# Two fp32 transformer blocks on one core: half of the weight remainders of 16 units made by an adding DMA from GpSimd's queue

## The chip, the cores and the metric

The kernel runs on 1 core of a Trainium2 chip. The metric is device time in microseconds (us), lower is better; the time of a kernel is the median of its runs.

## What is computed

Two blocks follow each other on one sequence of 256 tokens, model width 1024, all in fp32. The stretch that matters here is mixer 1, between the first and the second SwiGLU feed-forward of block one:

```python
proj = h @ w_in                       # c_q 256, c_kv 128, k_rope 32, conv_in 3*512, gates 2*1024
q  = rms_norm(c_q) @ w_uq;  kv = rms_norm(c_kv) @ w_ukv
q, k = per-head rms_norm, rope        # 8 heads, 64 + 32 wide
o_attn = causal softmax attention(q, k, v)
o_conv = gate_b * causal_conv3(gate_c * xv)
merged = sum(sigmoid(gate_logits) * (branches @ w_branch));  y = merged @ w_out
```

After it come the second feed-forward, then block two (attention of two kinds, an MLP, a gated embedding, a final norm).

## The kernel before, in words

**Weights.** The weights come from HBM in *units* of at most 128 x 2048 fp32 (1 MB). `Sync.load` puts unit i into one of four raw buffers (`raw`, slot i % 4, NR = 4). TensorE multiplies in fp32r, so each weight is split into a rounded part ("hi") and a remainder ("lo"). `Scalar.hi` copies both halves of a unit from `raw` into `ring[.., 0, ..]` as fp32r (two activations). `Vector.lo` makes `ring[.., 1, ..] = raw - hi`, one instruction for each half, p = 0 and p = 1. The ring has four slots too (NS = 4): `hi` of weight unit w waits until TensorE has used unit w - 4. Each 128x128 tile then takes three matmuls (`product`), and a tile of the second half waits for `("lo", w, 1)`. A raw buffer is loaded again when both remainders of its unit are made.

Units of a second kind ("ada") hold rows of the modulation matrix. They share the raw buffers; VectorE alone reads them (`Vector.ada`, line L205, tile `sb_junk`, two instructions for each).

**Order.** `Plan` writes one list of steps, and every engine runs its own steps of that list in order. `take_unit` issues `hi` and puts the unit's remainder pieces at the end of a list `pend`; `piece` takes the first piece of it out and puts it into the plan (the load that reuses the raw buffer is planned when the last piece of a unit is out). Pieces go out in four ways: `need` takes units up to three ahead of the one that TensorE begins, and before each of them empties `pend` down to AHEAD = 3 entries; `went` lets one piece go at each fourth tile (PACE = 4), if more than KEEP = 2 are waiting; `fill` lets one go at chosen places between other VectorE work; and `need` forces the pieces of the unit that TensorE is about to use.

```python
        if self.lead and self.tiles // PACE > before // PACE and len(self.pend) > KEEP and not self.hold:
            self.piece()
```

**Mixer 1.** Weight units 33 and 34 are c_q, c_kv and k_rope; 35 and 36 conv_in 1 and 0; three ada units; 37 queries (1536 wide), 38 keys and values (1024 wide); 39 conv_out 0; 40 and 41 conv_in 2 and 3; 42 conv_out 2; 43 to 50 the gates, with ada units ahead of 46, 47 and 48; then the branch and output matrices. GpSimd makes the normalising factors of c_q, c_kv and k_rope in small steps (`Gpsimd.c_factors`). VectorE's statistics of the heads (`head_sums`, `head_factors`) need those factors. They stand in the plan between the keys of unit 38 and the first tile of unit 39. In the plan before, the piece (unit 40, p = 0) stands ahead of these statistics (it goes out at the PACE place of the keys, where four pieces wait), and (unit 40, p = 1) directly behind them. From `conv_out 2` on, the heads' transposes (`turn_heads`, `turned_heads`) and then the attention (`scores_1`, `masked_1`, `exp_1`, `normal_1`, `turn_1`, `turned_1`) run tile by tile beside the projections.

A line number in the rows is mostly that of a helper: L193 ACT activation, L196 tensor_tensor, L217 matmul, L220 transpose.

Of the kernel before, what the change touches and what calls it, by code (L numbers as in the profile page):

```python
# [8 lines left out]
F32, F32R, I32, BF16 = mybir.dt.float32, mybir.dt.float32r, mybir.dt.int32, mybir.dt.bfloat16  # L9
# [4 lines left out]
NR, NS = 4, 4  # L14
# [100 lines left out]
ADA_3 = [5, 6, 9, 17]  # L115

PACE, AHEAD, KEEP = 4, 3, 2
TAKE_AFTER = (1, 2, 3)
SUMS_AT = (1, 3)

# [57 lines left out]
class Engine:  # L178
# [40 lines left out]
    def transpose(self, o, i, ident):  # L219
        return Issued(self.e and self.e.transpose(o, i, ident))  # L220

    def dma_start(self, o, i):
        return Issued(self.e and self.e.dma_start(o, i))


class Turn:
# [238 lines left out]
class Plan:  # L465
# [20 lines left out]
    def load(self):  # L486
        if self.loads < len(self.m.units):
            self.add("load", self.loads)
            self.loads += 1

    def take_unit(self):
        i = self.taken
        self.taken += 1
        kind, blocks = self.m.units[i]
        if kind == "ada":
            self.pend += [("ada", i, b, n) for b, (_, n, _, _) in enumerate(blocks)]
        else:
            w = self.m.windex[i]
            self.add("hi", i, w)
            self.pend += [("lo", i, w, p) for p in range(2)]  # L500

    def fill(self, n=1):
        for _ in range(0 if self.hold else n):
# [167 lines left out]
    def first_ffn(self):  # L671
# [28 lines left out]
        for k in range(8):  # L700
# [13 lines left out]
            for j in range(8):  # L714
                for i in range(2):
                    self.mm(128, "up", "f1", j, k, i, bk[j])
                if k == 7:
                    if j in TAKE_AFTER:
                        self.take_unit()
# [20 lines left out]
    def mixer_1(self):  # L740
# [113 lines left out]

        cut = M1_ORDER.index(("qkv", 0))
        run(M1_ORDER[:cut], SUMS_AT)
        ko = ko[0]

# [86 lines left out]
        self.in_tiles(KEYS_AT, head_keys)  # L945
        self.in_tiles(ATTENTION_AT, start)
        run(M1_ORDER[cut + 1:])
        self.finish_side()
        self.add("gcol", 1, 0.5)
# [363 lines left out]
class Sync(Program):  # L1313


    def run(self):
        steps = {"load_c": self.load_c, "load_con": self.load_con, "load_x": self.load_x, "load": self.load,
                 "load_rows": self.load_rows, "load_mask": self.load_mask, "load_tables": self.load_tables,
                 "bias_store": self.bias_store, "load_bias": self.load_bias, "load_p": self.load_p,
                 "store": self.store, "end": self.end}  # L1320
        for name, args in self.plan.steps:
            if name in steps:
                steps[name](*args)
# [15 lines left out]
    def load(self, i):  # L1339
        m, e = self.m, self.e  # L1340
        if i >= NR:
            kind, blocks = m.units[i - NR]
            if kind == "ada":
                e.wait_ge(*self.at("ada", blocks[-1][1]))
            else:
                e.wait_ge(*self.at("lo", m.windex[i - NR], 1))
        w = m.widths[i]
        src = m.wts[m.offs[i]:m.offs[i] + 128 * w].rearrange("(p w) -> p w", p=128)
        e.dma_start(m.raw[:, i % NR, 0:w], src).then_inc(*self.up(f"unit{i % NR}_in", ("unit", i), by=16))
# [521 lines left out]
class Scalar(Program):  # L1871


    def run(self):
        steps = {"hi": self.hi, "silu_c": self.silu_c, "square_0": self.square_0, "rbc": self.rbc, "h_hi": self.h_hi,
                 "silu": self.silu, "hid_hi": self.hid_hi, "rope_sin": self.rope_sin, "hx_hi": self.hx_hi,
                 "square": self.square, "shift_hi": self.shift_hi, "c_shift": self.c_shift,
                 "c_square": self.c_square, "c_hi": self.c_hi, "c_sums_out": self.c_sums_out,
                 "conv_shift": self.conv_shift, "conv_xs": self.conv_xs, "conv_gate_shift": self.conv_gate_shift,
                 "conv_hi": self.conv_hi, "gate_shift": self.gate_shift, "gate_tanh": self.gate_tanh,  # L1880
                 "q_out": self.q_out, "qr_out": self.qr_out, "v_out": self.v_out, "k_out": self.k_out,
                 "head_squares": self.head_squares, "heads_kr": self.heads_kr, "turned_heads": self.turned_heads,
                 "exp_1": self.exp_1, "turned_1": self.turned_1, "o_hi_1": self.o_hi_1, "merged_hi": self.merged_hi,
                 "shifts": self.shifts, "gate_silu": self.gate_silu, "kA_square": self.ka_square,
                 "vA_out": self.va_out, "qA_square": self.qa_square, "turned_2": self.turned_2, "exp_A": self.exp_a,
                 "turned_pA": self.turned_pa, "o_hi_A": self.o_hi_a, "B_out": self.b_out, "vB_out": self.vb_out,
                 "exp_B": self.exp_b, "turned_pB": self.turned_pb, "o_hi_B": self.o_hi_b,
                 "gate2_tanh": self.gate2_tanh, "sum_hi_2": self.sum_hi_2, "up_out": self.up_out, "down_out": self.down_out, "hid2_hi": self.hid2_hi,
                 "p_hi": self.p_hi, "ple_tanh": self.ple_tanh, "x_square": self.x_square, "x_out": self.x_out,
                 "final_square": self.final_square,  # L1890
                 "final": self.final}
        for name, args in self.plan.steps:
            if name in steps:
                steps[name](*args)

    def hi(self, i, w):
        m, e = self.m, self.e
        e.wait_ge(*self.at("unit", i))
        if w >= NS:
            e.wait_ge(*self.at("used", w - NS))  # L1900
        for p in range(2):
            a, b = m.half(w, p)
            e.activation(m.ring[:, w % NS, 0, a:b], m.raw[:, i % NR, a:b]).then_inc(
                *self.up("weights_hi", ("hi", w, p)))
# [442 lines left out]
class Vector(Elementwise):  # L2347
# [76 lines left out]
    def rsqrt(self, v, z, a, event):  # L2424

        e = self.e
        self.ts(z.bitcast(I32), v.bitcast(I32), -0.5, ALU.mult, 1597463007.0, ALU.add)
        s = 1.0
        for n in range(3):
            e.wait_ge(*self.last())  # L2430
            self.tt(a, z, z, ALU.mult)
            e.wait_ge(*self.last())
            self.tt(a, a, v, ALU.mult)
            e.wait_ge(*self.last())
            e.scalar_tensor_tensor(z, a, 3.0 * s * s, z, ALU.subtract, ALU.mult).then_inc(
                *self.up("vector_own", *([event] if n == 2 else [])))
            s = -2.0 * s ** 3
        assert s == Z_SCALE
# [654 lines left out]
class Gpsimd(Elementwise):  # L3093
# [1 line left out]
    steps_done = "pool_own"  # L3095

    def run(self):
        steps = {"token_factor": self.token_factor, "diagonal": self.diagonal, "c_factors": self.c_factors}
        for name, args in self.plan.steps:
            if name in steps:  # L3100
                steps[name](*args)

    def rsqrt(self, v, z, a, event):

# [182 lines left out]
```

## Time and profile before

| | |
|---|---|
| median of 3 runs | 1026.38 us (1023.08 to 1027.05) |
| the profiled execution | 1024.29 us |
| its span in the profile | 1022.5 us |
| TensorE (matmul) busy | 983.3 us, 96% |
| VectorE busy | 780.2 us, 76% |
| ScalarE busy | 534.1 us, 52% |
| GpSimd busy | 10.5 us, 1% |

The span is the stretch that the profiler's rows cover; the run's own time is 1.8 us more. A busy TensorE is one with a matmul in flight. Units 35 to 50 are used between about 225 us and 345 us of the span.

### The profile page before, as it was taken

How to read it: one execution, taken by the hardware profiler on the slowest of the kernel's cores; microseconds unless marked ns; L12 is line 12 of the kernel's file. 1: busy time of each engine (PE TensorE's matmuls, PEld its weight loads, DVE VectorE, ACT ScalarE, POOL GpSimd, SP SyncE). 2: the span in 40 equal slices, each digit the busy share in tenths (PEclk: the TensorE clock that was granted, in tenths of full speed). 3: DMA queues.
4: the chain of work that ended last, by engine and by line, in shares of the span. 5: the costliest groups of instructions: out<-in, count | busy, mean ns of one | idle time of the engine just before them, and what ended most of it. 6: DMA issues, size and time to landing. Idle time of an engine off the chain costs nothing.

```text
span 1022.5 us, 17350 instructions
## 1 busy us (share of the span) xinstructions
PE 983.3 (96%) x7020; PEld 917.1 (90%) x7020; DVE 780.2 (76%) x1446; ACT 534.1 (52%) x936; POOL 10.5 (1%) x32
## 2 busy tenths in 40 slices
PE   4999999998888999999999999999999999999996
PEld 3999998997887999999998988789999988988895
DVE  5999998978986787685877588556768877677665
ACT  4444654436376555353565445664555654455453
POOL 0000000004000000000000000000000000000000
PEclk9999999999999999999999999999999999999998
DMA  8997999854473555768664445354355555545421
GB/s 305 358 343 281 336 345 342 304 196 167 173 280 124 199 195 182 246 220 206 254 247 165 170 160 203 127 170 143 136 192 169 191 181 192 206 165 194 156 104 41
DMA packets 33277, 213.92 MB, mean 209 GB/s; under 512 B 3757, under 2 KB 6189, under 8 KB 8494
## 3 DMA queue, kind: packets, MB, share of 16 engines
q1 hardware_dynamic: 33198, 212.83, 58.8%
q8 instruction: 55, 0.90, 0.3%
q14 instruction: 24, 0.20, 0.0%
HBM read 210.19 MB, written 2.62 MB: 208 GB/s over the span
## 4 chain that ended last, share of the span: by engine, by line
PE 85%; DVE 7%; ACT 3%; issue 2%; DMA 1%; POOL 1%; SPq 0%; DVEq 0%; ACTq 0%; POOLq 0%
PE bank L217 84%; DVE sb_ring L196 2%; PE bank L220 2%; DMA sb_raw<-wts 1%; ACT sb_ring L193 1%; ACT sb_tmp L193 1%; DVE sb_tq L196 1%; DVE sb_tmp L202 1%; DVE sb_tmp L196 1%; DVE sb_junk L205 1%; ACT R L193 0%; DVE sb_nst L196 0%; DVE sb_tmp L199 0%; POOL sb_st_a L196 0%; DVE R L196 0%
## 5 line engine op out<-in xcount | busy, mean ns | idle before, releaser
L217 PE MATMUL bank<-sb_h,sb_ring 128*128 128x258 f32 (+2 forms) x3776 | 495.0, 291 | 8.7 <-DVE sb_ring L196 4.0
L217 PEld LDWEIGHTS bank<-sb_h,sb_ring 128*128 128x128 f32 x3776 | 474.1, 189 | 23.0 <-issue 4.8
L196 DVE TENSOR_TENSOR sb_ring<-sb_raw,sb_ring 128x1024 fp32r<-128x1024 f32 (+1 forms) x324 | 384.8, 1205 | 3.0 <-ACT sb_ring L193 3.0
L193 ACT ACTIVATE sb_ring<-sb_raw 128x1024 fp32r<-128x1024 f32 (+1 forms) x324 | 320.0, 1037 | 81.8 <-DMA sb_raw<-wts 49.4
L217 PE MATMUL bank<-R_512r,sb_ring 128*128 128x256 f32 (+1 forms) x1608 | 225.3, 301 | 0.0
L217 PEld LDWEIGHTS bank<-R_512r,sb_ring 128*128 128x128 f32 x1608 | 211.3, 188 | 11.9 <-issue 0.3
L217 PE MATMUL bank<-sb_ring,sb_h 128*128 128x512 f32 (+1 forms) x504 | 112.5, 378 | 0.0
L217 PEld LDWEIGHTS bank<-sb_ring,sb_h 128*128 128x128 f32 x504 | 87.4, 188 | 16.6
L205 DVE CUSTOM_DVE_ANT_0 sb_junk<-sb_raw,sb_csil,sb_cols 128x1024 bf16<-128x1024 f32 x72 | 92.3, 1282 | 2.8 <-DMA sb_raw<-wts 1.0
L217 PE MATMUL bank<-R_1024r,sb_ring 128*128 128x512 f32 (+1 forms) x576 | 91.8, 320 | 0.0
L217 PEld LDWEIGHTS bank<-R_1024r,sb_ring 128*128 128x128 f32 x576 | 82.0, 188 | 8.2
L196 DVE TENSOR_TENSOR sb_tq<-bank,sb_rbc 128x256 f32<-128x256 f32 x87 | 34.7, 421 | 62.0 <-ACT sb_zb L193 39.9
L193 ACT ACTIVATE R_512r<-sb_tq 128x256 fp32r<-128x256 f32 x60 | 25.1, 418 | 78.1 <-DVE sb_tq L196 51.0
L193 ACT ACTIVATE sb_tmp<-bank 128x256 f32<-128x256 f32 (+2 forms) x62 | 27.9, 461 | 29.7 <-PE bank L217 27.4
L193 ACT ACTIVATE sb_tmp<-sb_tmp,sb_smx 128x256 f32<-128x256 f32 (+2 forms) x40 | 21.0, 525 | 34.8 <-DVE sb_smx L205 24.6
L202 DVE SCALAR_TENSOR_TENSOR sb_x<-bank,sb_gcol,sb_x 128x256 f32<-128x256 f32 x36 | 17.3, 482 | 27.9 <-PE bank L217 27.4
L193 ACT ACTIVATE sb_h<-sb_x,sb_cols 128x256 fp32r<-128x256 f32 x24 | 14.2, 592 | 39.3 <-DVE sb_x L202 23.7
L193 ACT ACTIVATE sb_tq<-sb_tq,sb_zb 128x256 f32<-128x256 f32 x26 | 13.3, 510 | 31.7 <-DVE sb_tq L196 31.7
L196 DVE TENSOR_TENSOR R_512r<-sb_tq,R_512r 128x256 fp32r<-128x256 f32 x60 | 25.2, 420 | 3.9 <-ACT R_512r L193 3.9
L220 PE MATMUL bank<-sb_con,sb_tmp 128*128 128x128 f32 (+1 forms) x134 | 21.2, 276 | 6.4 <-ACT sb_tmp L193 4.2
L193 ACT ACTIVATE sb_tq<-bank 128x256 f32<-128x256 f32 (+1 forms) x35 | 12.9, 367 | 26.7 <-PE bank L217 26.7
L196 DVE TENSOR_TENSOR sb_tmp<-bank,sb_tmp 128x256 f32<-128x256 f32 x32 | 12.4, 425 | 18.6 <-ACT sb_tmp L193 18.6
(162 smaller groups left out, 560.3 us busy)
## 6 DMA issues: line engine op xcount, KB each, us to landing
sb_raw<-wts SPq DMA_DIRECT2D x193, 1024.0 KB, 4.9
sb_raw<-wts SPq DMA_DIRECT2D x3, 512.0 KB, 3.6
scratch<-R SPq DMA_DIRECT2D x1, 1536.0 KB
sb_x<-xt SPq DMA_DIRECT2D x2, 512.0 KB, 5.8
out<-R SPq DMA_DIRECT2D x2, 512.0 KB, 2.6
R<-scratch SPq DMA_DIRECT2D x2, 508.0 KB, 9.4
sb_raw<-wts SPq DMA_DIRECT2D x1, 768.0 KB, 4.4
sb_raw<-wts SPq DMA_DIRECT2D x1, 640.0 KB, 3.9
```

The source lines that it names most:

```text
L193: return Issued(self.e and self.e.activation(o, i, func, **kw))
L196: return Issued(self.e and self.e.tensor_tensor(*a))
L202: return Issued(self.e and self.e.scalar_tensor_tensor(*a))
L205: return Issued(self.e and self.e.tensor_tensor_reduce(*a))
L217: return Issued(self.e and self.e.matmul(o, w, m, start=start, stop=stop, skip_group_check=True))
L220: return Issued(self.e and self.e.transpose(o, i, ident))
```

## The change

For weight units 35 to 50 (`ADDED`) the remainder of the second half is not made by VectorE. ScalarE writes the negated rounded weights into `ring[.., 1, ..]` directly behind `hi`, and GpSimd issues a DMA that adds the raw half onto them. The first half stays with VectorE. So `take_unit` puts one piece for each of these units into `pend` in place of two. `Sync.load` waits for both halves.

```diff
+ADDED = range(35, 51)
...
             self.add("hi", i, w)
-            self.pend += [("lo", i, w, p) for p in range(2)]
+            if w in ADDED:
+                self.add("lo_added", i, w)
+                self.split.add((w, 1))
+            self.pend += [("lo", i, w, p) for p in range(1 if w in ADDED else 2)]
...
-                e.wait_ge(*self.at("lo", m.windex[i - NR], 1))
+                for p in range(2):
+                    e.wait_ge(*self.at("lo", m.windex[i - NR], p))
...
+    def lo_added(self, i, w):            # ScalarE
+
+        m, e = self.m, self.e
+        a, b = m.half(w, 1)
+        e.wait_ge(*self.at("hi", w, 1))
+        e.activation(m.ring[:, w % NS, 1, a:b], m.ring[:, w % NS, 0, a:b].bitcast(F32), scale=-1.0).then_inc(
+            *self.up("weights_negated", ("negated", w)))
...
+    def lo_added(self, i, w):            # GpSimd
+        m, e = self.m, self.e
+        a, b = m.half(w, 1)
+        e.wait_ge(*self.at("unit", i))
+        e.wait_ge(*self.at("negated", w))
+        e.dma_start(m.ring[:, w % NS, 1, a:b].bitcast(F32), m.raw[:, i % NR, a:b], accum_op=ALU.add).then_inc(
+            *self.up(f"rest{w % NS}_added", ("lo", w, 1), by=16))
```

## Rows read from the trace of the kernel before

**Rows 1.** Busy time by stretch: us, PE, PEld, DVE, ACT, POOL, PEclk, DMA share, GB/s

```profile
218.00:345.00 127.00, 113.50 (x886) 107.67 (x884) 103.67 (x227) 74.17 (x178) 10.31 (x28) 0.99 0.53 190
250.00:260.00 10.00, 5.95 (x40) 5.75 (x39) 9.51 (x29) 2.65 (x5) 0.00 (x0) 0.83 0.23 73
290.00:300.00 10.00, 10.00 (x85) 9.95 (x84) 8.59 (x16) 6.57 (x14) 0.00 (x0) 1.00 0.85 309
```

**Rows 2.** Timeline of PE in mixer 1; in brackets idle time before, and its releaser

```profile
243.85 8.81 PE L217 MATMUL bank<-sb_h,sb_ring 128*128 128x258 f32 x72
256.71 4.75 PE L217 MATMUL bank<-sb_h,sb_ring 128*128 128x258 f32 x27 [4.05 <-DVE sb_ring L196]
...
268.68 2.43 PE L217 MATMUL bank<-sb_h,sb_ring 128*128 128x258 f32 x18 [1.39 <-DVE sb_tq L196]
...
277.65 0.64 PE L220 MATMUL bank<-sb_con,R 128*96 128x128 f32 x4 [0.59 <-ACT R L193]
...
285.17 0.64 PE L220 MATMUL bank<-sb_con,R 128*96 128x128 f32 x4 [1.36 <-ACT R L193]
...
305.54 0.52 PE L220 MATMUL bank<-sb_con,sb_tmp 128*128 128x128 f32 x3 [1.29 <-DVE sb_tmp L199]
...
309.87 0.55 PE L220 MATMUL bank<-sb_con,sb_tmp 128*128 128x128 f32 x3 [0.65 <-ACT sb_tmp L193]
...
315.39 0.55 PE L220 MATMUL bank<-sb_con,sb_tmp 128*128 128x128 f32 x3 [1.78 <-ACT sb_tmp L193]
```

**Rows 3.** Timeline of DVE around the statistics of the heads

```profile
237.93 1.22 DVE L196 TENSOR_TENSOR sb_ring<-sb_raw,sb_ring 128x1024 fp32r<-128x1024 f32 x1
...
240.88 2.35 DVE L196 TENSOR_TENSOR sb_ring<-sb_raw,sb_ring 128x1024 fp32r<-128x1024 f32 x2
...
249.06 0.43 DVE L196 TENSOR_TENSOR sb_tmp<-R 128x256 f32<-128x256 f32 x1 [1.39 <-POOL sb_tq L196]
...
255.43 3.49 DVE L196 TENSOR_TENSOR sb_ring<-sb_raw,sb_ring 128x1024 fp32r<-128x1024 f32 x3
```

**Rows 4.** Timeline of POOL: steps of `c_factors`

```profile
236.58 0.20 POOL L196 TENSOR_TENSOR sb_st_v<-sb_tq,sb_con 128x4 f32<-128x4 f32 x1 [236.16 <-ACT sb_tq L193]
...
238.09 1.11 POOL L196 TENSOR_TENSOR sb_st_a<-sb_st_z 128x6 f32<-128x6 f32 x1
...
242.25 1.05 POOL L199 TENSOR_SCALAR sb_st_a<-sb_st_a 128x6 f32<-128x6 f32 x1
...
243.97 0.20 POOL L196 TENSOR_TENSOR sb_st_a<-sb_st_z 128x6 f32<-128x6 f32 x1
...
248.77 0.25 POOL L196 TENSOR_TENSOR sb_tq<-sb_tmp 128x32 f32<-128x32 f32 x1
```

**Rows 5.** Instruction groups by form in 218 to 340 us: the splitting of weights

```profile
L196 DVE TENSOR_TENSOR sb_ring<-sb_raw,sb_ring 128x1024 fp32r<-128x1024 f32 x28 | 33.5, 1219 | 0.0
L193 ACT ACTIVATE sb_ring<-sb_raw 128x1024 fp32r<-128x1024 f32 x28 | 27.9, 1046 | 0.1
```

**Rows 6.** Timeline of ACT: the rounded parts of units 36, 37, 39 and 50

```profile
211.70 2.00 ACT L193 ACTIVATE sb_ring<-sb_raw 128x1024 fp32r<-128x1024 f32 x2
224.22 1.58 ACT L193 ACTIVATE sb_ring<-sb_raw 128x768 fp32r<-128x768 f32 x2 [10.53 <-DMA sb_raw<-wts]
...
234.40 1.99 ACT L193 ACTIVATE sb_ring<-sb_raw 128x1024 fp32r<-128x1024 f32 x2
...
312.10 1.99 ACT L193 ACTIVATE sb_ring<-sb_raw 128x1024 fp32r<-128x1024 f32 x2
```

**Rows 7.** Timeline of DVE: both remainders of unit 36

```profile
217.41 2.35 DVE L196 TENSOR_TENSOR sb_ring<-sb_raw,sb_ring 128x1024 fp32r<-128x1024 f32 x2
```

**Rows 8.** DMA issues of the page: KB each, median us from issue to landing

```profile
sb_raw<-wts SPq DMA_DIRECT2D x193, 1024.0 KB, 4.9
sb_raw<-wts SPq DMA_DIRECT2D x3, 512.0 KB, 3.6
...
R<-scratch SPq DMA_DIRECT2D x2, 508.0 KB, 9.4
```

More of the change, by code:

```diff
@@ L220, in transpose, with dma_start @@
         return Issued(self.e and self.e.transpose(o, i, ident))
-    def dma_start(self, o, i):
-        return Issued(self.e and self.e.dma_start(o, i))
+    def dma_start(self, o, i, **kw):
+        return Issued(self.e and self.e.dma_start(o, i, **kw))
 class Turn:
@@ L1874, in run @@
     def run(self):
-        steps = {"hi": self.hi, "silu_c": self.silu_c, "square_0": self.square_0, "rbc": self.rbc, "h_hi": self.h_hi,
+        steps = {"lo_added": self.lo_added, "hi": self.hi, "silu_c": self.silu_c, "square_0": self.square_0, "rbc": self.rbc, "h_hi": self.h_hi,
                  "silu": self.silu, "hid_hi": self.hid_hi, "rope_sin": self.rope_sin, "hx_hi": self.hx_hi,
@@ L3097, in run @@
     def run(self):
-        steps = {"token_factor": self.token_factor, "diagonal": self.diagonal, "c_factors": self.c_factors}
+        steps = {"lo_added": self.lo_added, "token_factor": self.token_factor, "diagonal": self.diagonal, "c_factors": self.c_factors}
         for name, args in self.plan.steps:
```

## The prediction

> **What bounds the kernel now.** I read first the page's busy times: TensorE has a matmul in flight for 96% of the span, so VectorE work that is taken away is worth something only where TensorE waits for it. Next the busy times by stretch. Units 35 to 50 are used within 218 to 345 us, and there TensorE is busy for 113.5 of 127 us while VectorE is busy for 103.7 [rows 1]. So at most 13.5 us stand idle there, and that is the ceiling of any gain. Then TensorE's timeline, for where those 13.5 us lie [rows 2]. The largest piece is 4.05 us before 256.71, released by a VectorE instruction on the ring. The granted clock of 250 to 260 is 0.83 [rows 1], and the 27 matmuls behind this wait take 4.75 us where 72 before it took 8.81, which makes 3.3 for 27: another 1.4 us. Then 1.39, 0.59 and 1.36 us up to 285.17, and 1.29, 0.65 and 1.78 in the attention.
>
> Now VectorE's timeline beside it [rows 3]. From 249.06 (released by GpSimd) it computes the head statistics, and at 255.43 it comes to three remainders in a row, of which the first is unit 40's second half. TensorE had done 24 tiles from 243.85 on: unit 39 and the first half of unit 40. So TensorE waits for VectorE, VectorE waited for GpSimd, and GpSimd's chain began at 236.58, when ScalarE delivered its sums [rows 4].
>
> **What is removed and added.** VectorE loses 16 instructions, 14 of them of 1.22 us and two narrower [rows 5]: 17.1 us and at most 2.4 more, some 18.7. ScalarE gains 16 activations of a half each, 14 of 1.05 us and two narrower: some 16.1 us. GpSimd gains 16 DMAs, each of 512 KB of payload in 14 of 16 cases. These amounts lie beside a busy TensorE nearly everywhere; what counts is their place.
>
> **The place of unit 40's first half.** This is the step I hold the most important. The pending list gets one entry for a unit in place of two, but KEEP stays 2. Followed step by step: conv_in 0's fill takes unit 39's only piece; the queries take unit 40, one entry; the keys take unit 41, two entries. Two is not more than KEEP, so nothing goes out at the keys. Unit 42 makes it three, and (unit 40, first half) goes out at the fourth tile of unit 39, behind the head statistics. Today's second half stands exactly there, and the first half stands ahead of them, in the pair at 240.88 [rows 3]. So VectorE will not make the missing first half before it has done the statistics. TensorE then stops at the start of unit 40, not in its middle: at 243.85 + 16/24 of 8.81 = 249.7 instead of 252.7. It resumes at the same VectorE instruction and has 8 tiles more to do: **+2.9 us**. The adding DMA of unit 40 itself stands on GpSimd's queue behind `c_factors`, which end at 249.0 [rows 4]. It has until the middle of unit 40, some 10 us, so it costs nothing; without that cover TensorE would stand for the transfer.
>
> **The chain ahead of it.** ScalarE's negations of units 37, 38 and 39 come before its sums for `c_factors`: 37 directly behind the 1.58 us pair at 224.22, which the rest of its queue has waited for, and 39 behind the pair at 234.40 [rows 6]. The widths 768, 512 and 1024 make 0.8 + 0.6 + 1.05 = 2.4 us. GpSimd also issues unit 39's DMA before `c_factors`; that overlaps the sums, and I take 0.3 for it. Against this, three steps of `c_factors`, the first at 238.09 and the last at 242.25, took 1.05 to 1.11 us where the same kind takes 0.20 at 243.97 [rows 4]; all three coincide with remainders on VectorE (237.93, 240.88 and its second one [rows 3]). Two of the three remainders are no longer there: -1.7. Balance **+1.0 us** (bounds: 0, if VectorE's own relief in this chain absorbs one activation; 2.7, if the steps stay slow).
> The Trainium skill (SBUF — State Buffer, GpSimd and VectorE's shared port pair) says that a VectorE instruction with two SBUF inputs keeps a GpSimd instruction that reads SBUF waiting; by that rule, too, 1.7 us come back, and the 1.1 us against 0.20 agree.
>
> **Behind it.** VectorE has 8 remainders fewer between 255 and 299, where it is busy without a pause (8.59 of 10 us even in 290 to 300 [rows 1]). So the waits whose cause is its backlog go: 1.39 before 268.68 (bank not emptied), and 0.59 and 1.36 before 277.65 and 285.17, where ScalarE's turn came late because it had waited for VectorE [rows 2]. With 0.2 of a small one: **-3.5 us**. I leave the clock's 1.4 us as they are: TensorE will stand longer here, not shorter.
>
> **The attention.** ScalarE's pairs for units 49 and 50 stand ahead of `exp_1` and `turned_1`; the pair of unit 50 is at 312.10, and TensorE waits 1.78 us behind it [rows 2, 6]. One more activation each: +2 x 1.05, of which some 0.2 is absorbed. VectorE is freed of a piece ahead of `masked_1` of head 0 and so takes 1.0 of the 1.29 us before 305.54. **+0.9 us**. From unit 51 on nothing is changed.
>
> **The adding DMA as a gate for loads.** Raw buffers are now given back when the DMA has landed. Unit 36's rounded part ends at 213.7 [rows 6], negated at 214.7. The load of unit 37 goes today when VectorE is done at 219.8 (217.41 + 2.35) [rows 7], and lands at 224.2, for which ScalarE stands idle 10.5 us [rows 6]. VectorE's first half of 35 slips behind the norm's factor too and is now made at 217.41, and 36's behind it, so 219.8 holds. The DMA must take no more than 5.1 us from the negation to landing, or everything behind moves. By the same reckoning unit 46's DMA has some 4.3 us before it delays unit 48's load, at a DMA share of 0.85 [rows 1]. What does it take? No row shows one. From below a 512 KB load, 3.6 us; from above 9.4 us, the 508 KB transfers with short rows [rows 8]. It reads two operands, as many bytes as a 1024 KB load reads, which lands in 4.9 us; with an issue of about 1 us (a slowed GpSimd step) I take **6 us**. Cost: 0.9 at unit 37, 1.7 at unit 48, of which half reaches TensorE: **+1.8 us**. At 3.6 us nothing; at 9.4 us 4.3 + 5.1, at most +9.4.
> The Trainium skill (DMA: Bandwidth & Descriptors, "Anatomy of one DMA") gives 2.0 us + bytes / 436 GB/s for a DMA from GpSimd, an estimate of 3.2 us here; by that the term would be 0 and the sum 1.8 us lower. No row here shows such a DMA.
>
> **Sum.** 2.9 + 1.0 - 3.5 + 0.9 + 1.8 = **+3.1 us**. On the profiled execution's 1024.29 that is 1027.4; it stands 2.1 us under the median of the runs, so I forecast 1026.38 + 3.1 = **1029.5 us**, within 0.5% (5.1 us) of before, which is about what a measurement of this kernel can tell from no change. The likeliest case's own range, from the bounds of the chain (-1.0, +1.7) and of a DMA between 3.6 and 7 us (-1.8, +1.5), is 1026 to 1031.5.
>
> **Rivals.**
> (1) *Relief wins, faster.* If unit 40's first half were ready before 249.7, TensorE would pass without a stop: 4.05 + 1.4 gone, then 3.5, and 1.0 in the attention, less 1.9 for ScalarE: some -8, **1018 us**. For it: VectorE is the engine named before the largest wait. Against: the pending list, as followed. It decides at one place, whether that first half stands before or behind the statistics. A smaller gain could come from GpSimd's chain. Chance 0.12.
> (2) *The landing is slow.* With 9.4 us the two gated loads cost up to 9.4 in place of 1.8: +6 to +11, **1035 us**. For it: the DMA share of 0.85 where the gates are loaded, two operands read. Against: 0.53 on average. It decides from 5.1 us on. Chance 0.23.
> (3) *GpSimd's issuing is slow.* Its instructions stretched from 0.20 to 1.1 us beside VectorE. If an issue takes 3 us, unit 39's delays `c_factors` by 3, and the head statistics, and unit 40; each transfer is 2 us later: +4 to 5 on top of 3.1, **1034 us**. Against: one issue alone stands in that chain. Chance 0.13.
> The Trainium skill (SBUF — State Buffer, the "DVE blocks DMA" trap) says that GpSimd can't write its descriptors while VectorE runs a two-port instruction; that speaks for this rival. No row here shows descriptor writing.
> (4) *It doesn't do what it says:* the transfers slow the loads and VectorE's relief is given back, the stops being where they were. That is inside the forecast.
>
> **Chances.** Forecast 0.52, (1) 0.12, (2) 0.23, (3) 0.13. Faster by over 0.5%: 0.12; within: 0.52; slower: 0.36. Range 1020 to 1038: it leaves out the best part of (1) and the worst of (2), not quite 2 in 10.
>
> **What would show it.** Right: in TensorE's timeline a wait of 7 to 9 us at the start of unit 40, after 48 matmuls of conv_out 0 and none of conv_in 2, released by `sb_ring` on VectorE; `c_factors` beginning 2 to 3 us later and lasting 1 to 2 us less; no waits from 268 to 286; VectorE busy 18 to 19 us less, ScalarE 16 more. Wrong: an adding DMA landing under 4 or over 8 us, ScalarE idle for raw data at units other than 37, a GpSimd issue over 2 us, or a different order of VectorE's pieces around the statistics.

## The result

| | before | changed |
|---|---|---|
| median of the runs | 1025.72 us (4 runs) | 1034.57 us (4 runs) |
| profiled execution | 1024.29 us | 1035.28 us |
| its span | 1022.5 us | 1033.5 us |

The ratio is 1.0091, with an interval of 1.0071 to 1.0111: slower by 9.3 us. (One of the four runs, 1953.4 us, was disturbed: it counts in the median above and not in the ratio, and the other three lie within 1033.48 and 1035.28.) The time is inside the range given and beyond the likeliest case's own, on the side for which 0.36 was given.

The page of the changed kernel, busy us by engine, then the DMAs that GpSimd issues:

```profile
PE 990.5 (96%) x7020; PEld 923.3 (89%) x7020; DVE 763.5 (74%) x1430; ACT 551.1 (53%) x952; POOL 23.6 (2%) x48
...
q0 software_dynamic: 2304, 8.00, 4.1%
...
sb_ring<-sb_raw POOLq DMA_DIRECT2D x14, 512.0 KB, 6.4
```

The amounts are near those that were forecast: VectorE has 16.7 us less (18.7 forecast), ScalarE 17.0 more (16.1), and an adding DMA of 512 KB lands 6.4 us after its issue (median), against 4.9 for a load of twice the size [rows 8]. Busy time by stretch in the changed kernel (columns as in rows 1):

```profile
218.00:345.00 127.00, 109.84 (x804) 103.84 (x803) 82.17 (x200) 82.22 (x178) 21.54 (x42) 0.92 0.79 234
...
310.00:320.00 10.00, 8.76 (x56) 8.46 (x56) 5.43 (x26) 7.70 (x20) 1.01 (x1) 0.83 0.81 218
320.00:330.00 10.00, 7.10 (x36) 5.87 (x35) 3.44 (x11) 5.14 (x15) 1.01 (x1) 0.66 0.83 262
```

Against rows 1, VectorE goes from 103.7 to 82.2 busy us of 127, TensorE from 113.5 down to 109.8, ScalarE from 74.2 up to 82.2, and the DMA share from 0.53 to 0.79. The 127 us hold less of the work now (804 matmuls against 886), so not all of VectorE's 21.5 us are saved. The granted clock of the whole stretch is 0.92 against 0.99; in the kernel before, the two stretches of 10 us shown here both had 1.00:

```profile
310.00:320.00 10.00, 8.22 (x65) 7.44 (x66) 7.51 (x21) 6.69 (x21) 0.00 (x0) 1.00 0.43 156
320.00:330.00 10.00, 8.73 (x71) 7.95 (x69) 6.45 (x22) 6.15 (x17) 0.00 (x0) 1.00 0.29 105
```

TensorE's timeline in the changed kernel, in the places of rows 2:

```profile
235.86 0.31 PE L222 MATMUL bank<-sb_con,sb_tmp 32*128 32x32 f32 x2 [1.57 <-DVE sb_tmp L201]
...
241.29 7.24 PE L219 MATMUL bank<-sb_ring,R_512r 128*128 128x512 f32 x36 [0.54 <-ACT sb_tq L195]
248.37 5.93 PE L219 MATMUL bank<-sb_h,sb_ring 128*128 128x258 f32 x48
261.00 15.45 PE L219 MATMUL bank<-sb_h,sb_ring 128*128 128x258 f32 x114 [6.70 <-DVE sb_ring L198]
276.29 0.60 PE L222 MATMUL bank<-sb_con,R 128*96 128x128 f32 x4
...
288.51 0.65 PE L222 MATMUL bank<-sb_con,R 128*96 128x128 f32 x4 [0.24 <-ACT R L195]
...
294.99 0.64 PE L222 MATMUL bank<-sb_con,R 128*96 128x128 f32 x4 [0.33 <-ACT R L195]
...
305.13 0.92 PE L219 MATMUL bank<-R,R 96*128 96x256 f32 x4 [0.84 <-ACT R L195]
...
311.16 0.52 PE L222 MATMUL bank<-sb_con,sb_tmp 128*128 128x128 f32 x3 [1.93 <-DVE sb_tmp L201]
311.43 4.18 PE L219 MATMUL bank<-sb_h,sb_ring 128*128 128x258 f32 x21
...
323.07 0.90 PE L222 MATMUL bank<-sb_con,sb_tmp 128*128 128x128 f32 x3 [2.90 <-ACT sb_tmp L195]
...
325.38 4.53 PE L219 MATMUL bank<-sb_h,sb_ring 128*128 128x258 f32 x21
...
355.17 5.08 PE L219 MATMUL bank<-R_512r,sb_ring 128*128 128x256 f32 x41
```

TensorE's lag behind the kernel before, read by pairing landmarks: +4.5 us at the queries (236.76 before), +5.35 at the first transposes of the heads (270.94 before), +3.3 at the fifth ones (285.17 [rows 2]), +5.6 and +7.7 at the first and third `turn_1` (305.54, 315.39 [rows 2]), +10.4 at the end of mixer 1 (344.73 before). So 4.5 to 5.4 us are lost early, 2 are won back from 276 to 288, 1.6 are lost around the two new waits of 0.33 and 0.84 us (the lag at 308.41 is 5.0), and 5.5 in the attention. The stop at unit 40 is there as forecast: 48 matmuls of conv_out 0, none of conv_in 2, then 6.70 us for `sb_ring` (7 to 9 forecast). VectorE still releases the longest of these waits.

The chain of work that ended last says what stood ahead of each loss (start, us, what; stretches around 212 and 285 us):

```profile
212.10 1.91 ACT sb_ring L195 x2
214.03 1.07 ACT sb_ring L195
215.14 0.50 issue
215.64 5.27 DMA sb_ring<-sb_raw
220.98 5.27 DMA sb_raw<-wts
226.27 1.59 ACT sb_ring L195 x2
227.88 0.85 ACT sb_ring L195
...
239.86 1.07 ACT sb_ring L195
240.97 0.49 issue
241.46 0.86 POOL sb_ring L225
...
286.82 1.07 ACT sb_ring L195
287.94 0.49 issue
288.42 5.79 DMA sb_ring<-sb_raw
294.27 7.11 DMA sb_raw<-wts
301.40 2.02 ACT sb_ring L195 x2
```

Read downwards, the first block is the named gate: unit 36 rounded, negated, its DMA landed, and only then unit 37's load, so that ScalarE rounds unit 37 at 226.27 and not at 224.22 [rows 6]. (0.3 us of these 2.05 were there before: ScalarE began unit 36 at 212.01 and not at 211.70.) The single activations of 0.85 and 1.07 us are negations, and 241.46 is GpSimd's issue ahead of `c_factors`. The last block is the other gate: unit 46's landing, then unit 48's load in 7.11 us, for which ScalarE waits 2.81 us.

### The profile page after: what moved, and what is told of

Its sections match the earlier page's. It is cut to its first block, busy times and chain, and to the rows that moved or that the text cites. A ratio compares the mean times of both kernels' runs of the same rounds, so it can differ in the third digit from the quotient of the medians.

```text
span 1033.5 us, 17539 instructions
## 1 busy us (share of the span) xinstructions
PE 990.5 (96%) x7020; PEld 923.3 (89%) x7020; DVE 763.5 (74%) x1430; ACT 551.1 (53%) x952; POOL 23.6 (2%) x48
## 4 chain that ended last, share of the span: by engine, by line
PE 79%; DVE 6%; DMA 6%; ACT 6%; issue 2%; POOL 1%; SPq 0%; DVEq 0%; ACTq 0%; POOLq 0%
PE bank L219 77%; DMA sb_raw<-wts 4%; ACT sb_ring L195 3%; PE bank L222 2%; DVE sb_tq L198 1%; DVE sb_ring L198 1%; ACT sb_tmp L195 1%; DMA sb_ring<-sb_raw 1%; DVE sb_junk L207 1%; DMA R<-rows 1%; ACT R L195 0%; DVE sb_tq L204 0%; SPq L225 0%; DVE sb_nst L198 0%; DVE R L204 0%
## 5 line engine op out<-in xcount | busy, mean ns | idle before, releaser
L219 PE MATMUL bank<-sb_h,sb_ring 128*128 128x258 f32 (+2 forms) x3776 | 500.5, 293 | 10.4 <-DVE sb_ring L198 6.9
L219 PEld LDWEIGHTS bank<-sb_h,sb_ring 128*128 128x128 f32 x3776 | 479.6, 191 | 24.8 <-issue 12.5
L198 DVE TENSOR_TENSOR sb_ring<-sb_raw,sb_ring 128x1024 fp32r<-128x1024 f32 x308 | 366.9, 1206 | 3.6 <-ACT sb_ring L195 3.6
L195 ACT ACTIVATE sb_ring<-sb_raw 128x1024 fp32r<-128x1024 f32 (+1 forms) x324 | 320.4, 1038 | 87.8 <-DMA sb_raw<-wts 53.7
L195 ACT ACTIVATE sb_h<-sb_x,sb_cols 128x256 fp32r<-128x256 f32 x24 | 14.2, 593 | 39.6 <-DVE sb_x L204 24.0
L222 PE MATMUL bank<-sb_con,sb_tmp 128*128 128x128 f32 (+1 forms) x134 | 21.5, 279 | 8.4 <-ACT sb_tmp L195 4.6
L222 PEld LDWEIGHTS bank<-sb_con,sb_tmp 128*128 128x128 f32 (+1 forms) x134 | 15.8, 142 | 12.9 <-ACT sb_tmp L195 5.2
```

The costliest lines, as they stand in the source:

```text
L195: return Issued(self.e and self.e.activation(o, i, func, **kw))
L198: return Issued(self.e and self.e.tensor_tensor(*a))
L219: return Issued(self.e and self.e.matmul(o, w, m, start=start, stop=stop, skip_group_check=True))
```

## The experiments

"Before" is run beside each; ratios are to it, with 95% intervals. 1 us is 0.00098 of the time.

| run | median us | ratio | interval |
|---|---|---|---|
| piece moved forward, changed kernel | 1033.75 | 1.0080 | 1.0053 to 1.0106 |
| piece moved forward, kernel before | 1025.27 | 1.0006 | 0.9992 to 1.0020 |
| ScalarE's part alone | 1032.63 | 1.0077 | 1.0056 to 1.0098 |
| no negation | 1029.40 | 1.0045 | 1.0032 to 1.0058 |
| plain copy | 1032.26 | 1.0082 | 1.0067 to 1.0097 |
| without units 36 and 46 | 1031.43 | 1.0072 | 1.0048 to 1.0097 |
| units 41 to 45 only | 1024.24 | 0.9994 | 0.9979 to 1.0009 |
| ScalarE's part, units 35 to 39 | 1027.76 | 1.0036 | 1.0022 to 1.0051 |
| first half moved back, kernel before | 1025.00 | 1.0003 | 0.9994 to 1.0012 |
| units 41 to 45, piece moved forward | 1020.75 | 0.9965 | 0.9953 to 0.9977 |
| units 40 to 50 only | 1029.12 | 1.0038 | 1.0020 to 1.0055 |
| units 35 to 39 only | 1029.26 | 1.0045 | 1.0027 to 1.0063 |

### Is it the place of unit 40's half?

Three runs. In the first two one line is put ahead of the head statistics in `Plan.mixer_1`, in the changed kernel and in the kernel before:

```diff
+        self.piece()
         for n in range(3):
             for t in range(2):
                 b = tmp.take()
```

> The changed kernel, with one planned piece more: (unit 40, first half) goes out ahead of the head statistics on VectorE. Theory P (the place of that half is a large term): TensorE no longer stops at the start of unit 40; it stops in its middle until unit 40's adding DMA, issued at about 253.5 us behind c_factors, has landed at about 259.5 us, which is 261.0 + 2.9 - 259.5 = 4.4 us ahead of the changed kernel. Some of it is lost at the later gate, so about 1031 us against 1034.6. Rival G (landings gate the loads of units 37 and 48 and set everything behind them): the later gate takes it all back, 1033.5 to 1034.6 us.

> The kernel before, with the same one piece: here it is (unit 40, second half) that goes out ahead of the head statistics. Theory P: the wait of 4.05 us before 256.71 goes, and with it the 1.4 us at the lower clock; VectorE has 1.8 us of waiting for GpSimd there to hide the 1.1 us of work. About 1021 us against 1025.7. Rival B (VectorE's backlog behind the statistics sets the time, whichever half stands where): TensorE stops for banks or first halves a little later, 1024 to 1026 us.

In the changed kernel TensorE did pass the start of unit 40, waited 1.63 us in its middle for the DMA and was back to the kernel before at the heads' first transposes (271.17), a lag of 0.2 us in place of 5.35. Of these 5.1 us, 1.2 were there ahead of unit 40 already (queries at 240.10 against 241.29): this execution came into mixer 1 earlier. At the end the lag was 9.6 again, and the time no different from the changed kernel's. The chain of this run shows where it went:

```profile
284.10 1.07 ACT sb_ring L195
285.21 0.49 issue
285.69 10.61 DMA sb_ring<-sb_raw
296.37 6.95 DMA sb_raw<-wts
303.34 2.02 ACT sb_ring L195 x2
```

The gate opens no earlier than in the changed kernel (303.34 against 301.40): the DMAs and loads come closer together now, and unit 46's landing takes 10.61 us. So Rival G was right for this run; the interval alone (1030.2 to 1035.6 us) would not exclude Theory P's 1031. In the kernel before nothing was won either; TensorE's timeline there:

```profile
243.73 11.69 PE L217 MATMUL bank<-sb_h,sb_ring 128*128 128x258 f32 x96
258.94 0.63 PE L217 MATMUL bank<-sb_h,sb_ring 128*128 128x258 f32 x3 [3.52 <-DVE sb_tmp L196]
261.26 10.52 PE L217 MATMUL bank<-sb_h,sb_ring 128*128 128x258 f32 x63 [1.70 <-DVE sb_tmp L196]
```

It does all of units 39 and 40 (96 matmuls) and then stops for the banks that VectorE empties next: 3.52 + 1.70 in place of 4.05, 0.18 and 1.39. Behind them the granted clock of 260 to 270 is 0.66, and the 63 matmuls take 10.52 us, where at 1.00 72 take 8.81: 2.8 us lost, against 1.4 in the kernel before. That made me doubt the +2.9 of the prediction, and the third run moves the first half back, alone:

```diff
+        self.hold = True
         self.mm(1024, "keys", kn, v_b)
+        self.hold = False
```

> The kernel before with one piece moved the other way: (unit 40, first half) goes out behind the head statistics, as in the changed kernel, and nothing else is changed. VectorE then makes four remainders in a row there instead of three. Theory P (the place of that half costs a half unit of TensorE's head start): TensorE stops at the start of unit 40 for about 7 us and has 24 more matmuls to do behind it, +2.9 us, and +1.1 us for the fourth remainder in VectorE's backlog: 1027.5 to 1028.5 against 1024.5. Rival B (VectorE's chain of statistics and backlog sets the time there, and TensorE has its slack behind it, as the run with the second half moved forward suggests): the 2.9 us are absorbed by the bank wait of 1.39 us and others behind it; +0.5 to +1.5 us.

```profile
243.24 5.91 PE L217 MATMUL bank<-sb_h,sb_ring 128*128 128x258 f32 x48
255.39 15.76 PE L217 MATMUL bank<-sb_h,sb_ring 128*128 128x258 f32 x114 [6.24 <-DVE sb_ring L196]
270.99 0.60 PE L220 MATMUL bank<-sb_con,R 128*96 128x128 f32 x4
```

The stop looks as in the changed kernel, 6.24 us at the start of unit 40. Yet the heads' transposes come at 270.99 against 270.94 (with the queries at 236.18 against 236.76, so 0.6 us later counted from there), and the time is that of before within 1.2 us. Two things take up the 2.9 us of the eight tiles. The waits of 0.18 and 1.39 us for VectorE behind unit 40 are gone, 1.6 us. And `c_factors` take 11.6 us in place of 12.4, since one remainder fewer runs on VectorE beside them, so the head statistics end 0.8 us earlier.

### ScalarE's part alone, and the change without it

The kernel before, with the negation in `Scalar.hi` and this in `Vector.lo`:

```diff
+        if p and w in ADDED:
+            e.wait_ge(*self.at("negated", w))
+            e.tensor_tensor(m.ring[:, w % NS, 1, a:b], m.raw[:, i % NR, a:b], m.ring[:, w % NS, 1, a:b].bitcast(F32),
+                            ALU.add).then_inc(*self.up("weights_lo", ("lo", w, p)))
+            return
```

> ScalarE's part alone: the kernel before in its own order of pieces; ScalarE negates the second halves of units 35 to 50 as in the changed kernel, and VectorE adds the raw half onto them in place of subtracting (same length, same place). No DMA from GpSimd, VectorE not relieved. Theory S (the negations lie in chains that TensorE waits for: 2.4 us ahead of c_factors, 2 us ahead of the attention's softmax): +3.5 to +5 us over before, 1029.5 to 1031. Rival G (only the landing of the DMA costs): +0 to +1 us, 1026 to 1027.

The changed kernel without the negation:

```diff
-        steps = {"lo_added": self.lo_added, "hi": self.hi,
+        steps = {"hi": self.hi,
...
-        e.wait_ge(*self.at("negated", w))
+        e.wait_ge(*self.at("hi", w, 1))
```

> The changed kernel without ScalarE's negation: the DMA adds the raw half onto whatever the ring's slot holds, right behind the rounded part, so the remainders of those second halves are not the right numbers. Theory S: 4 to 5 us faster than the changed kernel, about 1030 us: the DMAs start 1.05 us earlier too. Rival G: only that 1 us of earlier start at each of two gates comes back, 1032.5 us.

ScalarE's negations alone cost 7.9 us, more than the 3.5 to 5 of Theory S, and without them the changed kernel keeps 4.6 us of its 9.3, as Theory S had it. In the second run the DMAs also start an activation earlier, so its 4.7 us are not the negations' alone. The two don't add up to 9.3 (7.9 + 4.6 = 12.5): in the first run VectorE is not relieved. TensorE's waits in the run with ScalarE's part alone:

```profile
238.87 7.22 PE L219 MATMUL bank<-sb_ring,R_512r 128*128 128x512 f32 x36 [1.73 <-ACT sb_tq L195]
...
280.85 0.64 PE L222 MATMUL bank<-sb_con,R 128*96 128x128 f32 x4 [1.73 <-ACT R L195]
...
288.80 0.64 PE L222 MATMUL bank<-sb_con,R 128*96 128x128 f32 x4 [1.84 <-ACT R L195]
...
315.07 0.55 PE L222 MATMUL bank<-sb_con,sb_tmp 128*128 128x128 f32 x3 [1.68 <-ACT sb_tmp L195]
...
321.68 0.82 PE L222 MATMUL bank<-sb_con,sb_tmp 128*128 128x128 f32 x3 [2.85 <-ACT sb_tmp L195]
```

Each wait that ScalarE releases has grown, by one activation at most: 0.59 and 1.36 to 1.73 and 1.84, 0.65 and 1.78 to 1.68 and 2.85 [rows 2]; one of 0.36 is new, before 295.28, and the queries are 2.1 us late. That makes 2.1 + 2.0 + 2.1 = 6.2; another 1.5 us come behind the last of them, where the clock of 320 to 330 is 0.83 and was 1.00.

With `ADDED = range(35, 40)` in the same kernel:

> ScalarE's part alone for units 35 to 39 only: the kernel before, with the negations of these five, and VectorE adding in place of subtracting. The run with all 16 was 7.8 us over before. By its trace TensorE was 2.1 us behind at the heads' first transpose (the negations ahead of c_factors), and the rest came later: here I expect +2 us, 1026.5 to 1027.5. Rival (a lag of 2 us at that place is absorbed by the slack behind it, and only the attention costs): +0 to +0.7 us.

+3.7 us. The trace has the 2.2 us at the heads' transposes, and no slack absorbs them; 1.5 more come between the third and the fourth softmax, where the clock is 0.96 and then 0.86 in place of 1.00. This was not expected, and it is within what one execution can show.

### What of the landing is the adding?

```diff
-        ... m.raw[:, i % NR, a:b], accum_op=ALU.add).then_inc(
+        ... m.raw[:, i % NR, a:b]).then_inc(
```

> The changed kernel with the same DMAs, waits and bytes written, but without the addition: the raw half is copied over the negated one, so the remainders of those second halves are not the right numbers. Theory A (the adding makes the landing long, since it reads two operands): the 512 KB DMAs land in about 4.5 us against 6.4, the loads of units 37 and 48 go 2 us earlier, the DMA share of 260 to 300 us is lower, and the time is 1030.5 to 1032 us. Rival: GpSimd's issue, the fixed part and the traffic of the loads make the landing; it stays above 5.5 us and the time stays at 1033.5 to 1035.

```profile
sb_ring<-sb_raw POOLq DMA_DIRECT2D x14, 512.0 KB, 4.8
```

4.8 us against 6.4, and the DMA share of 280 to 300 is 0.78 against 0.99: the addition costs 1.6 us a DMA and a fifth of the share in that stretch. Of the whole span's share these DMAs take 1.9% where the adding ones took 4.1%. ScalarE's wait for unit 48 falls from 2.81 to 1.84 us. The time is some 1 us less (8.4 over before against 9.3, intervals overlapping). The landing was right, the effect on the time less than Theory A had it.

Unit 37 shows why. Counted from ScalarE's start on unit 36, its load goes out after 8.1 us in the kernel before, 9.0 in the changed one and 8.1 here, where the copy of unit 36 landed in 3.4 us and holds up nothing. Yet the load lands after 12.5, 14.2 and 14.4 us. What is longer is the load itself: 4.4 us in the kernel before, 5.3 and 6.3 in the other two. In both of these another 1 MB load has just gone out (at 218.97 in the changed kernel, 218.57 here), the one that takes unit 35's raw buffer; in the kernel before it went at 214.30 and had landed at 219.16. It is late because unit 35's first half has slipped behind VectorE's work for the norm. So the lateness of unit 37 came with the order of VectorE's pieces and two loads side by side; the landing of unit 36 alone is not shown to cost anything.

### Which units?

`ADDED` without 36 and 46, then 41 to 45 only:

> The changed kernel without units 36 and 46, whose remainders stay wholly with VectorE: these are the two whose landing stood in the chain ahead of a load that ScalarE then waited for. Theory G (gated loads): ScalarE's waits for raw data at units 37 and 48 go back to those of before (10.5 and under 0.5 us), two negations fewer; 3 to 4 us faster than the changed kernel, 1030.5 to 1031.5. Theory S (ScalarE's queue): only the two negations count, and only one of them stands in a chain: 0.5 to 1 us, 1033.5 to 1034.

> The change for units 41 to 45 only: behind the sums for c_factors, used while VectorE has its backlog, and ahead of the attention's softmax. Theory P+S+G (place of the negations and landings decides, not their number): the chain up to unit 40 is that of before, the waits of 1.39, 0.59 and 1.36 us before 268.7, 277.7 and 285.2 mostly go: 1022 to 1024 us, 1 to 3 us faster than before. Rival (any use of the adding DMA costs, through the DMA traffic and ScalarE): 1026 us or more.

Without 36 and 46, unit 37 is rounded at 224.00 again, and unit 48 doesn't wait any more; but unit 47 now does, 2.03 us, and TensorE waits 1.84 behind it. About 2 us are won (the intervals overlap), less than Theory G's 3 to 4 and more than Theory S's 0.5 to 1. The first gate is gone, though this run doesn't tell by what: unit 35's first half is early again as well (its buffer's load goes at 213.82). The second gate moved to unit 47. With 41 to 45 only, TensorE was 2.7 us ahead of before at the fifth transposes and 1.7 at the end in the profiled execution (1022.52 us), but over ten runs the ratio is not to be told from 1.

Then the two ends separately, `range(40, 51)` and `range(35, 40)`:

> The change for units 40 to 50 only (11 of 16), as in the changed kernel otherwise. The chain ahead of c_factors is then that of before. By the traces so far the changed kernel lost 4.3 us up to unit 40, won about 2 back behind it and lost the rest in the attention. If the losses add up: 1034.6 - 4.3, and some of the gain lost to the gate at unit 48, so 1030 to 1031.5. Rival (slack: what is won ahead is waited for at the later gate, as in the run with the moved piece): 1032.5 to 1034.5.

> The change for units 35 to 39 only. ScalarE's part of it alone gave +3.7 us. With GpSimd's issue ahead of c_factors (+1.0), unit 36's landing ahead of unit 37's load (+2.0), and VectorE relieved of five half remainders (-1 to -1.5): 1029 to 1030 us. Rival (VectorE's relief makes up for its part): 1027 us, no more than ScalarE's part alone.

+3.9 and +4.6 us. Together 8.5, against 9.3 for both: within their intervals the losses add up, and nothing absorbs the early one. The late units cost less than expected, the early ones as expected. The profiled execution of the late units is the lowest of six (1025.77 us), so its trace shows little of the 3.9.

### A version that beats both

> The change for units 41 to 45 only, with (unit 40, second half) going out ahead of the head statistics. Alone, the moved piece changed nothing (TensorE stopped a little later, for banks that VectorE's conv_gate had to empty), and alone the change for 41 to 45 was not to be told from before. Together VectorE comes to conv_gate one to two remainders earlier: theory B gives 1021 to 1023 us, 1 to 3 us faster than before. Rival (landings and negations eat it up): 1024 us, not to be told from before.

1020.75 us, 0.9965 (0.9953 to 0.9977): 3.6 us faster than before. TensorE's timeline:

```profile
243.57 11.65 PE L219 MATMUL bank<-sb_h,sb_ring 128*128 128x258 f32 x96
258.30 6.25 PE L219 MATMUL bank<-sb_h,sb_ring 128*128 128x258 f32 x48 [3.07 <-DVE sb_ring L198]
...
268.20 0.60 PE L222 MATMUL bank<-sb_con,R 128*96 128x128 f32 x4
```

The heads' transposes are 2.7 us ahead of before (270.94). The five DMAs land in 4.8 us, VectorE reaches `conv_gate` at once behind the statistics, and no negation lies ahead of `c_factors` or in the softmax. The profiled execution is the slowest of the seven (1023.57 us): its lead is 2.0 us at the third `turn_1` (313.38 against 315.39) and 0.6 at the end of mixer 1, with a clock of 0.83 between 310 and 320. The 3.6 us rest on the times; where all of them lie, this trace doesn't show.

## Why the prediction was right and wrong

- **Total.** +3.1 forecast, +9.3 measured. It lies inside the range of 1020 to 1038 because the range was wide: the likeliest case was missed, even by its own bounds (-2.8 and +3.2 around 1029.5 give 1026.7 to 1032.7, where the text has 1026 to 1031.5). The direction and most of the places named were right; the terms below were too small, and one was not in the sum.
- **The chain ahead, +1.0: mis-sized, 4.2 measured.** This is the largest miss. `c_factors` began at 242.12 and not at 236.58 [rows 4], 5.5 us later: 2.05 from unit 37's late load (0.3 of it older), 2.6 from three negations (forecast 2.4), 0.9 from GpSimd's issue (forecast 0.3: it did not overlap the sums). They took 11.1 us in place of 12.4, so 1.3 of the forecast 1.7 came back, and VectorE reached unit 40's half 4.2 us later (259.64 against 255.43 [rows 3]). The runs with ScalarE's part alone, which have neither the load nor the issue in this chain, are 2.1 to 2.2 us late at the heads' transposes.
- **The place of unit 40's first half, +2.9: true for the stop, no cost in the end.** This was "the step I hold the most important". TensorE stopped where the prediction said. In the kernel before the same stop costs nothing measurable (0.3 us, within +-0.9). "It resumes at the same VectorE instruction and has 8 tiles more to do" is true, but 1.6 of the 2.9 us only take the place of the bank waits behind unit 40, and 0.8 are the speed-up of `c_factors` that the sum had counted elsewhere, half of its -1.7. In the sum the 1.39 before 268.68 stood under VectorE's relief; a later stop takes it away without any relief. In the changed kernel TensorE was 4.3 us late when it resumed (261.00 against 256.71) and 5.35 at the heads' first transposes, so the eight tiles added 1.1 there. With the first half moved forward the heads' transposes came 5.1 us earlier, 3.9 counted from the queries, and the wait for unit 48 took it back. Rival (1) hung on the same thought: with the first stop passed, the time did not fall.
- **Behind it, -3.5: right in kind, too large.** All of the waits named are gone or below 0.3 us, and the lag fell by 2.0 between the first and the fifth transposes. The 1.4 us of the clock stayed, as forecast (114 matmuls in 15.45 us, which would be 13.9 at the pace of the 8.81 for 72).
- **The attention, +0.9: mis-sized, 5.5 measured.** The two negations cost 1.0 and 1.1 us, as worked out. But the 1.0 credited to VectorE's relief didn't come: the wait before `turn_1` of head 0 grew from 1.29 to 1.93. And the granted clock fell to 0.83 and 0.66 behind the longer waits: groups of 21 matmuls that take 2.77 us took 4.18 and 4.53. The first of them cost nothing, since ScalarE's copy that the next transpose waited for ended at 316.40 and TensorE began it at 316.45. Around the second, from 323.07 on, the lag grew from 7.7 to 10.5 us: a term of 2.8 us that the sum did not have.
- **The landing, +1.8: right in its length, partly wrong in what it gates.** 6 us forecast, 6.4 measured; 3.6 and 9.4 as bounds held for the median, single ones took 9.90 and, with the piece moved, 10.61. Unit 37 was late by 1.7 us against 0.9 forecast, but a copy that landed in time left it as late. The step that failed there is "so 219.8 holds": it looked at unit 36's buffer, and the half of unit 35 that slips also delays a load, which then runs beside unit 37's. At unit 48 the landing did gate: ScalarE waited 2.81 us, TensorE 0.84 behind it, and 1.6 us of lag were added around it, one negation included.
- **Rivals (2) and (3)** had 1035 and 1034 us. That the time is near both is chance: the landing was 6.4 and not 9.4 us, and an issue took 0.86 us and not 3. The issues stayed at 0.85 to 1.0 us beside a busy VectorE. The Trainium skill's "DVE blocks DMA" trap (SBUF — State Buffer) is thus not seen here; whether any VectorE instruction beside them is of the kind that it means, no run tells. The 3.2 us that the Trainium skill gives for such a DMA (DMA: Bandwidth & Descriptors, "Anatomy of one DMA"; an estimate) is half of what the adding DMAs took. The plain copies took 4.8 in the median, and 3.4 for unit 36, where less ran beside it.
- **ScalarE as a free engine.** The sum had some 4.3 us for the negations (2.4 + 2.1 - 0.2); alone they cost 7.9. ScalarE was 58% busy in the stretch (74.17 of 127 [rows 1]) and looked free, but it stands in every chain there, in order: 17 us of its work were dearer than the 17 us taken from VectorE were worth.

Open: how much of the 9.3 us is the clock. It differs between executions of kernels that wait alike, and no run holds it fixed. The mean granted clock of a whole execution was 0.988 to 0.990 in the changed kernel and 0.992 to 0.996 in the kernel before; for the late units alone, the run at 0.994 took 1025.77 us and the one at 0.990 took 1031.85.

## What to carry to other kernels

Work that is put on an engine with idle time is not hidden if that engine releases the waits: count how often the added instruction stands directly ahead of something that the bound engine waits for, and price it there in full. Before charging a stop its own length, ask what the next wait behind it was hiding; the part of it that takes the place of a later wait costs nothing. And when a buffer is freed later, look at the load that waits for it and at the loads that it will then run beside. Here only the relief of five units of sixteen, outside such chains, cost nothing, and it paid once a piece of VectorE's order was moved as well.

## What the runs showed of the hardware

An adding DMA from GpSimd, SBUF to SBUF, 512 KB: 6.4 us from issue to landing in the median, a plain copy of the same bytes 4.8. The adding ones took 5.2 and 4.8 where only five are issued, and 10.61 in a stretch where the DMA share was 0.83. The issue holds GpSimd for 0.86 us, that of most plain copies for 0.53. 8 MB of payload took 4.1% of the DMA engines' time over the span when added, 1.9% when copied. With the 16 adding DMAs the share in 218 to 345 us rose from 0.53 to 0.79, and 1024 KB loads in 205 to 350 us took 5.9 us in place of 4.9.
